# Strassen weight sums of a macaron encoder: all four made by GpSimd, none by VectorE

## The reference

```python
def swiglu(h, w_gate, w_up, w_down):
    return (jax.nn.silu(h @ w_gate) * (h @ w_up)) @ w_down

for l in range(DEPTH):
    x = x + 0.5 * swiglu(rmsnorm(x, norm_ffn1[l]), ffn1_gate[l], ffn1_up[l], ffn1_down[l])
    ...
    x = x + 0.5 * swiglu(rmsnorm(x, norm_ffn2[l]), ffn2_gate[l], ffn2_up[l], ffn2_down[l])
```

## Time and profile before

| | |
|---|---|
| median of 3 runs | 2697.14 us (2694.12 to 2697.91) |
| the profiled execution's own time | 2699.51 us |
| its span in the profile | 2697.5 us |
| granted TensorE clock | 0.999 |
| TensorE busy | 2682.3 us, 99% |
| VectorE busy | 1864.0 us, 69% |
| ScalarE busy | 1097.7 us, 41% |
| GpSimd busy | 210.1 us, 8% |

### The profile page before, as it was taken

The page is one execution under the profiler, slowest core; times in us unless marked ns, Lnnn a source line. Parts: engine busy times, 40 slices in busy tenths (PEclk is TensorE's granted clock), DMA queues, the critical chain, the costliest instruction groups (busy, mean ns, idle before and its releaser), DMA issues.

```text
span 2697.5 us, 40423 instructions
## 1 busy us (share of the span) xinstructions
PE 2682.3 (99%) x15690; PEld 2410.0 (89%) x15690; DVE 1864.0 (69%) x2358; ACT 1097.7 (41%) x1521; POOL 210.1 (8%) x99
## 2 busy tenths in 40 slices
PE   9999999999999999999999999999999999999999
PEld 6899989999998888999989999899999888889998
DVE  7888864555555457888878888554655554688886
ACT  5344344454443233433434433453544432334333
POOL 3111100000000000211001120000000000001110
PEclk9999999999999999999999999999999999999999
DMA  7432243222224333233222322322222243323321
GB/s 233 141 102 93 78 134 97 75 83 87 71 64 131 98 106 109 94 114 106 92 87 101 109 93 82 129 92 81 79 91 66 64 137 98 105 94 125 101 93 55
DMA packets 287216, 269.22 MB, mean 100 GB/s; under 512 B 12980, under 2 KB 267105, under 8 KB 286573
## 3 DMA queue, kind: packets, MB, share of 16 engines
q1 hardware_dynamic: 281896, 257.25, 30.5%
q0 software_dynamic: 4576, 6.34, 0.8%
q10 hardware_dynamic: 646, 4.31, 0.4%
HBM read 261.31 MB, written 12.49 MB: 102 GB/s over the span
## 4 chain that ended last, share of the span: by engine, by line
PE 96%; DVE 2%; DMA 1%; issue 1%; ACT 0%; POOL 0%; SPq 0%; DVEq 0%; ACTq 0%; POOLq 0%
PE proj L522 24%; PE proj L524 24%; PE proj L523 24%; PE acc L522 6%; PE acc L523 6%; PE acc L524 6%; PE acc L711 1%; PE acc L733 1%; PE acc L772 1%; DMA raw<-in_ffn_up 1%; PE acc L720 0%; PE acc L571 0%; POOL cos_sin L496 0%; DVE ring_lo L1493 0%; PE acc L713 0%
## 5 line engine op out<-in xcount | busy, mean ns | idle before, releaser
L522 PE MATMUL proj<-h_hi,ring_hi 128*128 128x512 f32 (+1 forms) x1664 | 575.2, 346 | 3.1 <-DVE work L1547 3.1
L524 PE MATMUL proj<-h_hi,ring_lo 128*128 128x512 f32 (+1 forms) x1664 | 568.4, 342 | 0.0
L523 PE MATMUL proj<-h_lo,ring_hi 128*128 128x512 f32 (+1 forms) x1664 | 568.2, 341 | 0.0
L522 PE MATMUL proj<-y_hi,ring_hi 128*128 128x256 f32 (+1 forms) x1376 | 427.6, 311 | 0.0
L524 PE MATMUL proj<-y_hi,ring_lo 128*128 128x256 f32 (+1 forms) x1376 | 426.8, 310 | 0.0
L523 PE MATMUL proj<-y_lo,ring_hi 128*128 128x256 f32 (+1 forms) x1376 | 426.7, 310 | 0.0
L522 PEld LDWEIGHTS proj<-h_hi,ring_hi 128*128 128x128 f32 x1664 | 317.1, 191 | 39.3 <-issue 4.6
L524 PEld LDWEIGHTS proj<-h_hi,ring_lo 128*128 128x128 f32 x1664 | 316.9, 190 | 36.1
L523 PEld LDWEIGHTS proj<-h_lo,ring_hi 128*128 128x128 f32 x1664 | 317.2, 191 | 32.8
L1049 ACT ACTIVATE ring_hi<-raw 128x1024 fp32r<-128x1024 f32 (+1 forms) x175 | 223.9, 1281 | 295.4 <-PE acc L524 210.0
L522 PE MATMUL proj<-ring_hi,h_hi 128*128 128x384 f32 (+1 forms) x1024 | 335.3, 327 | 0.4 <-DVE work L1745 0.4
(11 more groups left out here) (239 smaller groups left out, 4020.4 us busy)
## 6 DMA issues: line engine op xcount, KB each, us to landing
raw<-in_ffn_gate SPq DMA_DIRECT2D x88, 512.0 KB, 3.9
raw<-in_ffn_up SPq DMA_DIRECT2D x88, 512.0 KB, 4.4
raw<-in_w_in SPq DMA_DIRECT2D x76, 512.0 KB, 4.6
raw<-in_ffn_down SPq DMA_DIRECT2D x56, 512.0 KB, 4.1
work<-in_ffn_down SPq DMA_DIRECT2D x32, 512.0 KB, 5.9
raw<-in_w_in SPq DMA_DIRECT2D x48, 320.0 KB, 4.1
raw<-in_w_in SPq DMA_DIRECT2D x48, 192.0 KB, 3.0
raw<-in_w_in SPq DMA_DIRECT2D x32, 256.0 KB, 3.5
```

Of the source, the lines that this page charges most:

```text
L522: pe.matmul(o, s_hi, m_hi, start=start, stop=False)
L523: pe.matmul(o, s_hi, m_lo, start=False, stop=False)
L524: return pe.matmul(o, s_lo, m_hi, start=False, stop=stop)
```

## The change

`t2` and `t4` of every group leave VectorE's program. GpSimd makes them behind `t1` and `edge` of the same group, with waits of its own: `t2` when the previous group's piece 3 is split, `t4` when its piece 5 is split and `b21` has landed. For the first group of an FFN the waits are on the splits of the activation operands (`op_lo_ready`), which use the same parts of `work`. `t1` now waits until the previous `t4` is done, which its own program order gives anyway. Semaphore `t_ready` counts as before, but GpSimd raises it.

```diff
@@ -492,11 +492,23 @@
                     if n:
                         pool.wait_ge(weights_lo, item + 2)
-                        pool.wait_ge(t_ready, 2 * (FAST * F4 + n - 1) + 1)
+                        pool.wait_ge(t_ready, 2 * (FAST * F4 + n - 1) + 2)
                     pool.tensor_tensor(t1_sum, b12, b11, ALU.subtract).then_inc(edge_ready, 1)
                     pool.wait_ge(edge_ready, 2 * (FAST * F4 + n) + 1)
                     pool.wait_ge(ffn_landed[1][1], 16 * (q + 1))
                     pool.tensor_tensor(b12, b22, b12, ALU.subtract).then_inc(edge_ready, 1)
+                    if n:
+                        pool.wait_ge(weights_lo, item + 4)
+                    else:
+                        pool.wait_ge(op_lo_ready, 7 * F4 + 4)
+                    pool.tensor_tensor(t2_sum, t1_sum, b22, ALU.subtract).then_inc(t_ready, 1)
+                    pool.wait_ge(t_ready, 2 * (FAST * F4 + n) + 1)
+                    pool.wait_ge(ffn_landed[0][1], 16 * (q + 1))
+                    if n:
+                        pool.wait_ge(weights_lo, item + 6)
+                    else:
+                        pool.wait_ge(op_lo_ready, 7 * F4 + 7)
+                    pool.tensor_tensor(t4_sum, t2_sum, b21, ALU.add).then_inc(t_ready, 1)
...
-                def t2(i, g):
-                    dve.wait_ge(edge_ready, 2 * (FAST * F4 + 2 * i + g) + 2)
-                    dve.tensor_tensor(t2_sum, t1_sum, b22, ALU.subtract).then_inc(t_ready, 1)
-
-                def t4(i, g):
-                    dve.wait_ge(ffn_landed[0][1], 16 * (g0 + PLAIN + 2 * i + g + 1))
-                    dve.wait_ge(t_ready, 2 * (FAST * F4 + 2 * i + g) + 1)
-                    dve.tensor_tensor(t4_sum, t2_sum, b21, ALU.add).then_inc(t_ready, 1)
...
                     gate_lo(0)
                     piece_lo(i, 1, 2)
-                    t2(i, 1)
                     silu_low(0)
...
                     hidden_hi(0)
-                    t4(i, 1)
                     hidden_lo(0)
...
                         for m in range(4):
                             add_down(e, D, m, PAIR_BANKS)
-                        t2(i + 1, 0)
-                        t4(i + 1, 0)
```

More of the change, by code:

```diff
@@ L1702, in ffn @@
                 add_down(1, 20, 6, PLAIN_BANKS)
-                t2(0, 0)
                 add_down(1, 20, 7, PLAIN_BANKS)
-                t4(0, 0)
                 with dve.Fori(0, PAIRS - 1) as i:
```

## The result

The changed kernel takes 2758.01 us (median; 2755.72 to 2761.78), against 2696.14 us of the kernel before in the same comparison: a ratio of 1.023, 95% interval 1.0217 to 1.0243. It is slower by 62 us; I had forecast 2757.

The account below looks back on a forecast made before the run. TensorE, busy 2682.3 of 2697.5 us, bounds the kernel. Terms 4 x 1.9 + 12 x 1.0 + 12 x 2.2 + 3 x 2.2 - 2 = 50.6 us, plus 9 for low clock: 60 on 2697.14, 2757; range 2718 to 2785.

Parts of the forecast that it names:

- The port: VectorE instructions with two SBUF inputs and GpSimd instructions reading SBUF exclude each other; a sum holds VectorE up to 2.3 us.
- The turns: When both engines wait, they alternate: GpSimd ends 2.26 us after VectorE's instruction, VectorE's 0.55 to 2.15 us after GpSimd's.
- Second group of a pair: Odd n: `c12` (L1578) ends 2.56 us later; TensorE's second product waits 1.0 us, 1.9 in an FFN's first pair.
- First group of the next pair: Even n: sums fall at the end of the current pair, delaying its last y_lo; TensorE waits 2.2 us in 12 places.
- First group of an FFN: Second plain down part: 2.2 us wait in each of the later three FFNs; first FFN nothing or the same; `t4` nothing.
- What is gained: VectorE reaches piece 2 of an FFN's first pair some 0.5 us earlier, removing short `u3` waits: -0.5 x 4 at most.
- The clock: Behind some TensorE waits, 3.4 us at 1.2 GHz costs 1.5 us; taken 6 times, 9 us, from 0 to 19 possible.
- The lower clock behind nearly every wait: Rival: TensorE's low clock follows 14 to 19 waits, 21 to 28 us, giving 2769 to 2776; chance 0.16.
- one wait of two being real: Rival: only one of a pair's waits, for `c12` or last y_lo, occurs: 15 to 38 us, 2712 to 2735; chance 0.17.
- room at the port: Rival: GpSimd's sums slip into gaps of VectorE's SBUF use and nothing waits: 2695 to 2700; chance 0.05.
- a gain: Rival: VectorE, 1.13 us earlier at two places, removes three `u3` waits of 3.1 us and their low clock: 2692.5; chance 0.02.
- a starved GpSimd: Rival: VectorE's stream starves GpSimd's four sums, pieces 3 and 5 come late, some 3 us more per group: above 2790; chance 0.04.

Follow-up runs that it names:

- the two fill kernels: Changed kernel with GpSimd writing zeros into `t2` and `t4` instead of sums, one fill or three in a row for each sum: 2696.23 and 2695.05 us.
- the pair of runs with sums and with fills: The changed kernel, GpSimd making `t2` and `t4`, 2758.01 us; the same with zero fills in place of these sums, 2696.23 us (one each) or 2695.05 us (three).
- the run with three fills: Changed kernel with each of `t2` and `t4` replaced by three zero fills in a row, each waiting for the one before: 2695.05 us, ratio 0.9998.
- the even groups held longer: Against the kernel before, only even groups' sums on GpSimd, held until the last y_lo is made and their own pieces 0 and 1 are split: 2695.16 us.
- the even groups alone: Against the kernel before, GpSimd makes `t2` and `t4` only for the first group of each pair (even n, group 0 too): 2739.44 us, ratio 1.0163.
- group 0 alone: Against the kernel before, GpSimd makes `t2` and `t4` only for group 0 of each FFN: 2706.58 us, ratio 1.0043.
- odd groups alone: Against the kernel before, GpSimd makes `t2` and `t4` only for the second group of each pair (odd n): 2715.64 us, ratio 1.007.
- the even groups held: Changed kernel, all sums on GpSimd, but `t2` of an even group waits for the last y_lo of the group before: 2713.97 us, ratio 1.0066.

## Why the prediction was right, point by point

**What bounds the kernel.** Right. TensorE had nothing to win: with 62 to 65 us less on VectorE and at most 0.7 us of new waits (the two fill kernels) the time is the same, with intervals of 0.1% to each side.

**The port.** Right, and shown by the pair of runs with sums and with fills. The turns held to 0.02 us. GpSimd's busy time of 397.3 was as forecast (near 400); VectorE's, forecast about as high as before, rose by 52.

**Second group of a pair.** The step is right, and one part of its size is off. Steady pairs wait 0.8 to 1.4 us (forecast 1.0); the 1.9 of the first pair came out as 0.2 to 0.8, because I worked it out without the effects of the change on the pair's own start. Alone it is 1.86.

**First group of the next pair.** 2.1 us in 12 places for 2.2 forecast. Held away from there, it costs nothing.

**First group of an FFN.** 2.2 us in the later three as forecast, but the first FFN isn't covered: 1.8 us (1.59 idle) before the matmul at 103.04. The steps there, from the two timelines: VectorE's two y_lo at 82.03 take 5.70 us instead of 3.50, the split behind them ends 1.3 us later, SyncE issues the last plain down rows at 89.96 instead of 88.71 while TensorE runs 0.9 us earlier than before, ScalarE splits them at 94.61 instead of 93.40, and the y_lo that follow are late. I had looked for a wait of TensorE beside the sums and not for a transfer that is issued behind them. The three rows that start this:

```profile
82.99 3.50 DVE L1513 TENSOR_TENSOR y_lo<-work,y_hi 128x512 fp32r<-128x512 f32 x2
```
```profile
82.03 5.70 DVE L1525 TENSOR_TENSOR y_lo<-work,y_hi 128x512 fp32r<-128x512 f32 x2
```
```profile
103.04 0.47 PE L534 MATMUL acc<-y_hi,ring_hi 128*128 128x512 f32 x1 [1.59 <-DVE y_lo L1525]
```

(The first is before's, the other two the changed kernel's.) `t4` of that group, which the forecast had put at nothing, isn't free either: beside it the split of piece 0 takes 3.13 us instead of 1.21, and the add that frees the first product's bank stands behind it in VectorE's program (0.8 us in 4 places).

**What is gained.** The short waits for `u3`, 0.6 us each, did go, here and in every kernel in which VectorE no longer makes the `t4` of group 0. The 2.3 us one went in this trace, but it isn't a property of the kernel: in the run with three fills one of 2.3 us stood in the first FFN, followed by its low-clock stretch, and the execution took 2698.79 us where the median is 2695.05. A single profiled execution had shown me one such case as if it were fixed. Of the 40 executions of the kernel before beside the experiments only 5 show a mean clock below 1.000, and 2 of 11 do with the even groups held longer. The prediction also says of the 2.4 us by which the profiled execution was above the median that they lie in no place that I change. That reading was wrong: the earlier trace rows show 2.3 us of waiting for `u3` and 1.5 of low clock in one place, at the sum that the change was to bring forward.

**The clock.** I took 6 stretches at 1.5 us, 9 us; there were 8 at 1.6, less the one of before: 11.3. The profiled execution was the slowest of the four, at a mean clock of 0.995; the others had 0.996 and twice 0.997, which with 3.4 us for each stretch makes 4 to 7 of them (an estimate). So 6 was a fair number for the median, by luck. The choice of a number between 0 and 19 was an estimate, and the trace gives the share: half of the waits for a y_lo, none of those of 1.4 us or less. The earlier trace rows told rightly that such a wait can bring a low clock. By the page of the Trainium skill that the prediction weighed ("TensorE: Matmul & The Clock Gate", "Why this matters for your kernels") the sum would have been 50.6, and the eight stretches stand against it.

**The total** is nearer than its parts, and that is luck: 4 us too much for `c12`, 1 too much for y_lo and 1.6 too little taken off for `u3` stand against 5 too little for the head of each FFN and 2 for the clock.

**The rivals.** The lower clock behind nearly every wait (14 or more) didn't come; one wait of two being real, room at the port, a gain and a starved GpSimd are each against the traces above (TensorE waits for no piece in any of them).

## What to carry to other kernels

Moving work from a busy engine to an idle one pays only if the two don't share what the work needs. Look in the trace for an instruction of the busy engine that is longer when the idle one runs: here 1.43 us instead of 0.69 told beforehand that the sums would hold VectorE, and the order of the program told where.

What a blocking instruction costs is decided by what stands beside it. The same 64 sums cost 62 us, 18 us or, half of them, nothing, by where the added waits put them; so write the order forward to the next deadline of the bounding engine, and include the transfers that are issued behind a delayed instruction.

When a sum of waits is set against a median, take from it only the waits that every execution has.

## What the runs showed of the hardware

A fill by GpSimd of 128 x 1024 (0.96 us), which reads nothing from SBUF, doesn't slow VectorE's instructions with two SBUF inputs (0.69 and 1.22 us, as alone), while a sum that reads SBUF stops them for its whole length. That a write alone is free was new to me in a trace; the Trainium skill states it in "SBUF — State Buffer", section "Who interferes with whom", and these rows agree.

Waits of TensorE of one length are followed in one and the same execution by 3.4 us at 1.2 GHz or by none: of the twelve with 1.96 or 1.97 us idle in the changed kernel six. Of all waits for a y_lo it is 8 of 16 there, 3 of 16 with the even groups alone, 1 of 4 with group 0 alone. The shortest that brought one was 1.85 us idle; none of the 36 with up to 1.70 us idle in the kernels with odd groups alone and with the even groups held did. What decides between two equal waits stays open; it wasn't tried.
